# Products of token rows: weights and their rests as one operand of 512 columns, added on the way out of the bank

## What is computed

```python
# first block, h = rmsnorm(x)
u = h @ w_in                                   # holds gla_k (256 columns), gla_v (512), ...
o = gla_chunked(heads(gla_q), heads(gla_k), heads(gla_v), heads(gk))
# second block, h = rms_norm(x), retention and attention
v, rv = h @ w_in_2 (columns of v), h @ w_in_2 (columns of rv)
# cross attention
mk, mv = split(mem_h @ w_mkv, 2)               # mem_h: 256 rows, mv: 1024 columns
o = softmax(q k) @ v
```

## Time and profile before

| | |
|---|---|
| median of 3 runs | 1830.45 us (1828.51 to 1830.47) |
| the profiled execution | 1829.16 us |
| its span | 1827.3 us |
| granted TensorE clock, mean | 0.995 |
| TensorE multiplying | 97% of the span, 11215 products |
| VectorE, ScalarE, GpSimd busy | 45%, 35%, 30% |
| products by tokens, L455 to L457 | 3 x 640, 0.28 us each |
| products by halves, L414 to L416 | 3 x 192, 0.28 to 0.31 us each |

### The profile page before, as it was taken

One profiled execution on the slowest core, in us unless ns is written; L12 is line 12 of the kernel. 1 busy time (PEld: TensorE's weight loads), 2 busy tenths in 40 slices (PEclk: granted clock), 3 DMA queues, 4 the chain that ended last, 5 costly groups with the idle time before them and its releaser, 6 DMA issues. The chain is left out here.

```text
span 1827.3 us, 27728 instructions
## 1 busy us (share of the span) xinstructions
PE 1772.7 (97%) x11215; PEld 1308.1 (72%) x11215; DVE 816.3 (45%) x1590; ACT 638.9 (35%) x1311; POOL 542.6 (30%) x411
## 2 busy tenths in 40 slices
PE   7999999999999999999999999998999999999998
PEld 5899989888897777778889778985973443533533
DVE  5677565334323554264461463324333434344333
ACT  5642343333243544453452365534421010100110
POOL 3342244546544542381562232352200000000000
PEclk9999999999999999999999999999999999999999
DMA  5220123223132111360432222225249999999997
GB/s 164 93 75 26 48 79 93 70 81 104 47 123 83 50 59 47 114 219 10 136 103 79 82 89 62 75 93 195 105 179 373 423 418 424 423 424 424 423 423 298
DMA packets 134548, 312.28 MB, mean 171 GB/s; under 512 B 15744, under 2 KB 102416, under 8 KB 111632
## 3 DMA queue, kind: packets, MB, share of 16 engines
q1 hardware_dynamic: 134416, 310.45, 45.4%
HBM read 308.33 MB, written 2.10 MB: 170 GB/s over the span
## 5 line engine op out<-in xcount | busy, mean ns | idle before, releaser
L321 POOL TENSOR_TENSOR unit_low<-unit_ring,unit_high 128x512 fp32r<-128x512 f32 x332 | 443.2, 1360 | 666.8 <-ACT unit_high L314 666.7
L360 PE MATMUL dense<-hT,unit_high 128*128 128x512 f32 x496 | 196.4, 396 | 2.1 <-DVE hT L2571 1.5
L314 ACT CAST unit_high<-unit_ring 128x512 fp32r<-128x512 f32 x332 | 186.8, 620 | 28.6 <-PE dense L362 22.5
L362 PE MATMUL dense<-hT,unit_low 128*128 128x512 f32 x496 | 193.5, 390 | 0.0
L361 PE MATMUL dense<-hT,unit_high 128*128 128x512 f32 x496 | 193.2, 389 | 0.0
L455 PE MATMUL dense<-unit_high,hT 128*128 128x256 f32 x608 | 175.5, 289 | 2.3 <-POOL unit_low L321 2.1
L456 PE MATMUL dense<-unit_low,hT 128*128 128x256 f32 x608 | 172.0, 283 | 0.0
L457 PE MATMUL dense<-unit_high,hT 128*128 128x256 f32 x608 | 171.9, 283 | 0.0
L4756 DVE TENSOR_TENSOR x<-x,side 128x512 f32<-128x512 f32 x128 | 81.7, 683 | 100.8 <-PE side L4581 99.3
L455 PEld LDWEIGHTS dense<-unit_high,hT 128*128 128x128 f32 x608 | 116.5, 192 | 9.6 <-POOL unit_low L321 2.9
L4544 PE MATMUL gate_sums<-expert_slot,xT 128*64 128x512 f32 x512 | 116.8, 597 | 0.0
(11 more groups left out here) (685 smaller groups left out, 3560.7 us busy)
## 6 DMA issues: line engine op xcount, KB each, us to landing
expert_slot<-w_exp_gate SPq DMA_DIRECT2D x60, 1024.0 KB, 15.5
expert_slot<-w_exp_down SPq DMA_DIRECT2D x60, 1024.0 KB, 16.3
expert_slot<-w_exp_up SPq DMA_DIRECT2D x58, 1024.0 KB, 16.0
unit_ring<-w_in SPq DMA_DIRECT2D x55, 1024.0 KB, 5.2
unit_ring<-w_mkv SPq DMA_DIRECT2D x8, 1024.0 KB, 5.4
unit_ring<-w_br SPq DMA_DIRECT2D x14, 512.0 KB, 6.2
expert_slot<-w_exp_up SPq DMA_DIRECT2D x12, 512.0 KB, 5.1
x<-x SPq DMA_DIRECT2D x8, 512.0 KB, 5.8
```

Of the source, the lines that this page charges most:

```text
L314: nc.scalar.copy(high[:, at:at + 512], raw[:, at:at + 512]).then_inc(*self.rounded.up())
L321: nc.gpsimd.tensor_tensor(low[:, at:at + 512], raw[:, at:at + 512], high[:, at:at + 512], ALU.subtract).then_inc(*self.split.up())
L360: nc.tensor.matmul(out, high[:, k, c], rh, start=(k == 0), stop=False)
L362: last = nc.tensor.matmul(out, low[:, k, c], rh, start=False, stop=(k == kd - 1))
```

## The change

A new method tile_by_parts takes one tile at a time to one bank. For each k the weights and their rests pass as one moving operand of 512 columns, in two pieces that lie apart in memory, into the two halves of the bank; the rest of the activations times the weights is accumulated to the right half. join_parts reads the left half with a copy on ScalarE and adds the right half on VectorE. The arrays low and high become slots of one array, so that one access pattern can name a slot of each. dense_gla for gla_k and gla_v, dense_mem_v and dense_tokens use the two. The places of ring.round move with it.

```diff
+        at = core.nc.sbuf_base - self.SLOTS * self.WIDTH * 4
+        core.sb(stack, "unit_high", [P, self.HIGHS, self.WIDTH], F32R)
+        self.rounds = core.nc.alloc_sbuf_tensor_at("unit_parts", [P, self.SLOTS + self.HIGHS, self.WIDTH], F32R, offset=at)
+        self.low, self.high = self.rounds[:, 0:self.SLOTS, :], self.rounds[:, self.SLOTS:, :]
...
+    def pair(self, n):
+        at, k, c = self.place(n, 0)
+        low, high = n % self.SLOTS, self.SLOTS + n % self.HIGHS
+        return self.rounds[:, low:high + 1:high - low, at:at + k * c].rearrange("p i (k c) -> p i k c", k=k)
+
+    def tile_by_parts(self, n, t, src):
+        nc = self.core.nc
+        self.round_rest(n)
+        high, pair = self.parts(n, 0)[0], self.pair(n)
+
+        def emit(bank, pe):
+            halves, s = bank[:].rearrange("p (i c) -> p i c", i=2), slice(t * P, (t + 1) * P)
+            for k in range(KD):
+                if t == 0:
+                    pe.wait_ge(*self.ready[n, 0, k])
+                nc.tensor.matmul(halves, src[:, 0, k, s], pair[:, :, k, :], start=(k == 0), stop=False)
+                last = nc.tensor.matmul(bank[:, 256:512], src[:, 1, k, s], high[:, k, :], start=False, stop=(k == KD - 1))
+            return last
+        return self.fill(emit)
...
+    def join_parts(self, bank_fill, out, form=None, **sizes):
+        bank, token, b = bank_fill
+        left, right = (bank[:, a:a + 256] for a in (0, 256))
...
+        @self.core.section.scalar
+        def _(act):
+            act.wait_ge(*token)
+            self.core.nc.scalar.copy(out, left).then_inc(*self.core.afree.up())
+        kept = self.core.afree.now()
+
+        @self.core.section.vector
+        def _(dve):
+            dve.wait_ge(*kept)
+            self.core.nc.vector.tensor_tensor(out, out, right, ALU.add).then_inc(*self.core.vfree.up())
         self.free[b] = self.core.vfree.now()
         return self.free[b]
...
@@ dense_gla
+            if halves:
+                at = {"gla_k": 256, "gla_v0": 0, "gla_v1": 256}[name]
+                for i in range(2):
+                    got = ring.tile_by_parts(n, 2 * f + i, S.hT)
+                    S.v_ready = ring.join_parts(got, (v if name[4] == "v" else qk)[:, 2 * f + i, at:at + 256])
+                    if i == 0:
+                        yield
+                ring.round(2)
...
@@ dense_mem_v
-        if i < 2:
-            halves = ring.tokens_by_half(n, (0, 1), memT)
-            next(halves)
+        for t in range(2):
+            S.chunk["mem_v", i] = ring.join_parts(ring.tile_by_parts(n, t, memT), v[i][:, t, :])
             ring.round(2)
-            yield
-            got = rest_of(halves)
-            ring.round(2)
-        else:
-            got = ring.tokens(n, (0, 1), memT)
-            ring.round(4)
-        S.chunk["mem_v", i] = ring.by_vector(got, lambda dve, bank: nc.vector.tensor_copy(v[i][:], bank[:].rearrange(
-            "p (t n) -> p t n", t=2)))
+            if i < 2 and t == 0:
+                yield
@@ dense_tokens
-            got = ring.tokens(n, (2 * f, 2 * f + 1), S.hT)
+            dst, form, sizes = out(i, f)
+            for t in range(2):
+                S.chunk[name, i, f] = ring.join_parts(ring.tile_by_parts(n, 2 * f + t, S.hT), dst[:, t], form, **sizes)
             ring.round(2)
-            dst, form, sizes = out(i, f)
-            S.chunk[name, i, f] = ring.by_scalar(got, lambda act, bank: nc.scalar.copy(dst, bank[:].rearrange(form, t=2, **sizes)))
```

More of the change, by code:

```diff
@@ L244, in __init__ @@
         self.ring = core.sb(stack, "unit_ring", [P, self.SLOTS, self.WIDTH])
-        self.low = core.nc.alloc_sbuf_tensor_at("unit_low", [P, self.SLOTS, self.WIDTH], F32R,
-                                                offset=core.nc.sbuf_base - self.SLOTS * self.WIDTH * 4)
-        self.high = core.sb(stack, "unit_high", [P, self.HIGHS, self.WIDTH], F32R)
+        at = core.nc.sbuf_base - self.SLOTS * self.WIDTH * 4
+        core.sb(stack, "unit_high", [P, self.HIGHS, self.WIDTH], F32R)
+        self.rounds = core.nc.alloc_sbuf_tensor_at("unit_parts", [P, self.SLOTS + self.HIGHS, self.WIDTH], F32R, offset=at)
+        self.low, self.high = self.rounds[:, 0:self.SLOTS, :], self.rounds[:, self.SLOTS:, :]
         self.tails = [core.nc.sbuf_base - (self.HIGHS - i) * self.WIDTH * 4 + 8 * KB for i in range(-self.SLOTS, self.HIGHS)]
@@ L471, in _ @@
             read(dve, self.bank[b]).then_inc(*self.core.vfree.up())
+        self.free[b] = self.core.vfree.now()
+        return self.free[b]
+    def join_parts(self, bank_fill, out, form=None, **sizes):
+        bank, token, b = bank_fill
+        left, right = (bank[:, a:a + 256] for a in (0, 256))
+        if form:
+            left, right = left.rearrange(form, **sizes), right.rearrange(form, **sizes)
+        @self.core.section.scalar
[7 more added lines that the diff above has]
+            self.core.nc.vector.tensor_tensor(out, out, right, ALU.add).then_inc(*self.core.vfree.up())
         self.free[b] = self.core.vfree.now()
@@ L1850, in dense_gla @@
         for f in range(2):
-            got = (yield from ring.tokens_by_half(n, (2 * f, 2 * f + 1), S.hT)) if halves else ring.tokens(n, (2 * f, 2 * f + 1), S.hT)
+            if halves:
[6 more added lines that the diff above has]
+                ring.round(2)
+                if name == "gla_k":
+                    S.qk_ready = S.v_ready
+                if f == 1:
+                    ring.finish(n)
+                yield
+                continue
+            got = ring.tokens(n, (2 * f, 2 * f + 1), S.hT)
             ring.round(2)
@@ L4044, in block_two @@
         dense_channels(core, ring, S, "mix_rqk", range(1, 2), lambda c: rk[:, c - 2, :], 64 ** -0.5),
-        dense_tokens(core, ring, S, "mix_rv", lambda i, f: (rv[:, 2 * f:2 * f + 2, i * 256:(i + 1) * 256], "p (t n) -> p t n", {})),
-        dense_tokens(core, ring, S, "mix_v", lambda i, f: (v[:, 2 * f:2 * f + 2, 4 * i:4 * i + 4, :], "p (t h d) -> p t h d", dict(h=4))),
+        dense_tokens(core, ring, S, "mix_rv", lambda i, f: (rv[:, 2 * f:2 * f + 2, i * 256:(i + 1) * 256], None, {})),
+        dense_tokens(core, ring, S, "mix_v", lambda i, f: (v[:, 2 * f:2 * f + 2, 4 * i:4 * i + 4, :], "p (h d) -> p h d", dict(h=4))),
         dense_z(core, ring, S, "mix_rg", z, temps, True))
```

## The result

The changed kernel takes **1837.81 us** (median of 5 runs, 1835.75 to 1840.98) against 1830.45 (1828.51 to 1831.3) of the kernel before: 7.4 us slower. The ratio on record is 1.0044, with a 95% interval of 1.0033 to 1.0055; the two medians alone give 1.0040. The forecast was 1830.8 within 1826.5 to 1836.5, with no change beyond 0.2% the likeliest. The time lies above the range, and it went slower by more than 0.2%, which had 0.24.

What follows compares the result with a forecast made beforehand. TensorE's own instructions, busy 97% of the span, were taken to set the time; -3.8 us saved and the added waits summed to +0.35 us, giving a median of 1830.8 us, range 1826.5 to 1836.5.

Steps and rivals of the forecast that it cites:

- (4): Rounding moved behind both copies, pieces late: +0.9 us at mix_rv and mix_v, +0.7 before gla_v1, +0.5 before gla_v0.
- (3): VectorE's new adds delay what follows: +0.8 us behind gla_k's first two tiles, +0.2 at the delta rule's scaled tiles.
- R4: Rival, chance 0.13: VectorE and GpSimd slow one another where moved roundings meet VectorE's chains; +3.8 us on the sum, 1834.6 us.
- (1): Step of k with the 512-column operand: 346.6 ns instead of 360.0, one fixed part of 13.3 saved; -3.8 us over 288 steps.
- R3: Rival, chance 0.10: the break in the wide product's moving operand costs 27 ns at each of 288 products; 1838.5 us.
- R1: Rival, chance 0.02: weight loads count in full, so each step saves 0.17 us, 49 us in all; 1781 us.
- R2: Rival, chance 0.13: the wide product hides the next load whole, 1823.1 us, or the late-piece and chain waits fail to appear, 1827.2.
- R5: Rival, chance 0.05: the fixed part is not per instruction, so nothing is saved and only waits remain, +4.15; 1834.6 us.
- (2): Way out by a copy and an add per tile: +0.25 us at retention's rv, otherwise nothing.
- (5): mem_v in the attention: add and VectorE's maximum behind it move later; between +0.3 and +1.0 us, taken as +0.5.
- (6): Gain lost where TensorE waits for another chain right after (attention, memory queries), about 20 of 288 steps: +0.3 us.
- The clock: Sign: a TensorE clock below 1.0 after a new wait would add time the sum has nowhere; no size or chance given.

Runs made afterwards that it cites:

- e9: Kernel before, with only the rounding of the next two pieces recorded behind the pair's copy in the three gla units: 1835.58 us, ratio 1.0027.
- e4: Changed kernel with the next unit's rounding put ahead of the first tile's copy in all three callers, adds kept in place: 1830.48 us, ratio 1.0003.
- e5: e4 with each wide product reading 512 contiguous elements of rounded weights, no break: 1921.31 us whole (it computes other values); step of k 353.6 ns.
- e3: Changed kernel with gla_k and gla_v as in the kernel before, only mixer rv, v and mem_v changed: 1830.38 us, ratio 1.0004.
- e2: Changed kernel with only the gla tiles changed, mixer rv, v and mem_v as in the kernel before: 1839.41 us, ratio 1.0054.
- e7: Changed kernel with the rounding put ahead of the first tile's way out at gla_k's first pair alone: 1835.41 us, ratio 1.0027.
- e8: Changed kernel with only the two adds of gla_k's first pair put off until the ladder's third double step: 1837.11 us, ratio 1.0040.
- e10: e4 with mem_v's eight tiles back to three products and one copy a pair: 1830.90 us, ratio 1.0009.
- e1: Changed kernel with gla_k's first two tiles the old way (three products, one bank, one ScalarE copy): 1834.98 us, ratio 1.0032.
- e6: e4 with gla_k's first pair's adds put off to the ladder's third double step and mem_v the old way: 1830.31 us, ratio 1.0000.

## Why the prediction was wrong

**The step that failed is the price of the moved rounding, (4) with (3).** It counted lateness: pieces that are not ready when a unit starts, 2.1 us in all. That part was right in kind and somewhat overpriced: TensorE waited 1.3 us for L344 (0.8 beside gla_v0 and gla_v1, forecast 1.2; 0.5 in retention, forecast 0.9). What it left out is where GpSimd's 2.5 us land once they are late: beside the ladder's chain and beside the scaled tiles, when TensorE waits for VectorE, instead of inside a fill. The prediction took VectorE's undisturbed times for the ladder (0.34 us from one operation to the next), although in the kernel before the pieces stretch a mask and a subtraction of the same ladder to 1.01 and 1.51 us at 148.77 and 149.71; only the fill hid that. I had this as R4, the rival with the right mechanism, at 0.13, and priced it at one operation for each of four places, 3.8 us, from the one slow L1188 of the earlier trace rows. In fact two operations are hit at a place, by 1.07 and 0.52 in the ladder and by about 1 us each at a scaled tile. In (3) I put it at 0.2, in the ladder at nothing. What the runs showed in its place: the place of the rounding alone costs 5.7 us (e9), and with it put back the changed kernel is within 1 us of the kernel before (e4).

- (1) The step of k: right in sign, two thirds in size. 8.6 ns saved in the mean instead of 13.3, so 2.5 us instead of 3.8: the sum was 1.3 too favourable here. The break in the operand (R3) costs nothing, as taken (e5). Some fills take the 346.6 ns of the sum to the digit, most take 353; that a fixed part of 13.3 ns is left per product holds for the former alone. The trace contradicts R1 and R2, and R5 in so far as something is saved. The remainder does not go away where the stationary operand stays the same: L415 has that of L414 ahead of it, loads it again, and starts 120.0 ns behind it like the others. The Trainium skill (TensorE: Matmul & The Clock Gate, Back-to-back issue gap) gives N/2.4 + 2.5 ns for a product alone; by that a step would be an estimated 325 ns. The trace, with 346.6 to 353.7, disagrees for these products, each of which loads weights, after as before.
- (2) rv's way out: TensorE's wait for rv went from 0.8 to 1.0 us, as said (+0.25).
- (3) The add in VectorE's order: right, and shown alone by e4: L1140 1.52 us after the fill, its waits 2.5 us instead of 1.6, that is +0.9 against +0.8.
- (4) mix in retention: the lag stays at 8.3 to 8.4, so its gain of about 1.1 us (128 steps) and its waits cancel; in e4 it falls by 0.5. Of the forecast waits of 0.9 us, 0.5 came.
- (5) mem_v in the attention: +0.6 in the changed kernel, 1.5 in e3 and e4, against +0.5. The wait moved to the scores: from 1075 to 1115 us the changed kernel's scores (L3768) wait 3.1 us for VectorE's neg_max and the next products (L3816) 0.6 for probsT, where before the scores (L3718) waited 0.7 and the next products (L3766) 2.7.
- (6) can't be told from the rest.
- The clock: the forecast named it as what the sum had nowhere, and gave it no chance. Of the 4.9 us that the changed kernel's profiled execution lost in the ladder, 2.3 have come by 157.6 (times of the kernel before), with the waits for L1140; 1.7 more come by 159.6, at half clock; 0.9 come behind that and are not placed.

The sum by what was measured, between the profiled executions of the changed kernel and e4: beside gla_v 3.6 lost against 0.6 gained (4.2 us), in the ladder 4.9 against 0.8 (4.1, half clock included), 8.3 in all. The medians lie 7.4 and 0.9 us over the kernel before, 6.4 apart. Beside gla_v the changed kernel's lag rises by 1.1, 1.1 and 0.8 us at 201, 210 and 221 (times of the kernel before). There TensorE waits first 0.5 for pieces and 0.3 for the scaled tile (kb), then 1.1 for kb, then 0.3 for pieces: 2.2 of 3.0, late pieces and stretched operations both. The wait for y adds little: the lag rises by 1.3 there and falls by 1.0 right behind it, where the kernel before waits for L1542. Open is why e9 loses less than the changed kernel: the medians lie 5.7 and 7.4 us over before, and the intervals (3.1 to 6.8, 6.0 to 10.1) overlap.

With the rounding ahead of the way out again the change is worth nothing that can be measured, 1.0003 (0.9994 to 1.0012): about 2.4 us less on TensorE, 0.9 more in the ladder's waits, and up to 1.5 in the attention. No version here beats the kernel before.

## What to carry to other kernels

When a code change moves where background work is issued, ask what the other engine does at the new time, not only whether the work is still ready in time: here a GpSimd subtraction of 2.5 us stretches VectorE's operations of 0.42 and 0.69 us to as much as 1.51 and 1.82, and that cost nothing while TensorE had a fill to run, and several us once TensorE waited for these operations. A slow row beside background work in the old trace is the warning, even where nothing waits for it. The cheap test is to move that one line alone in the kernel before (e9), and to move it back in the changed one (e4). Price a merged product by the distance between starts of the same mix of sizes, and read it in several fills: here one and the same step took 346.6 ns in some and 353.6 in others.

## What the runs showed of the hardware that was not expected

- Stretches of 3 to 8 us at the 1.2 GHz level come behind waits of TensorE, but not in every execution. Behind gla_k's first pair the changed kernel, e2, e3, e7, e8, e9 and e10 had one and the kernel before, e1, e4, e5 and e6 had none, and e3 runs the kernel before's instructions there. TensorE's busy time ahead of it does not tell them apart: 1.47 of 3 us in e4, which kept its clock, 1.61 in e10 and 2.40 in e3, which lost it. Each is worth some 1.3 (e6, 182 to 201 us) to 2.3 us (e10 against e4), so one profiled execution can't show a gain of 1 us.
- A moving operand of 512 columns in two pieces 12288 elements apart costs the same as a contiguous one (353.6 ns a step in both, in the same fill).
- A step of a 512-column and a 256-column product, each with its own weights' load, takes one of two values through a whole fill, 346.6 to 348.0 or 352.0 to 353.7 ns; single sizes add up to 347.3 (227.3 + 120.0). The kernel before, with 256-column products alone, has one value, 359.5 ns for three.
- VectorE and GpSimd can slow one another where they run side by side, in the kernel before as in the changed one: a VectorE operation of 128x256 took up to 1.51 us instead of 0.42, one of 128x512 up to 1.82 instead of 0.69, and GpSimd's two pieces up to 3.37 instead of 2.54. Not every operation is slowed: those that are here read both inputs from SBUF, while L1140, which reads one from a PSUM bank, took 0.41 us at 154.97, in the middle of GpSimd's subtraction.
